# A two-layer streaming encoder step: latents projected among the index scores, index queries in 416 columns, gates and projections placed elsewhere

## The reference

```python
h = rmsnorm(x, g_norm) * (1 + scale) + shift
z = h @ w_in   # cq, ckv, kr, ga, qb, kb, vb, qi, ki, wi, gb, ma, mb
q = (rmsnorm(cq, g_qnorm) @ w_uq)               # latent attention (MLA) queries
kn, va = mla_expand(rmsnorm(ckv, g_kvnorm), w_ukv)
score = jnp.einsum('bqhd,bsd->bqhs', qi, ki)    # index scores, 8 heads
idx_score = jnp.einsum('bqh,bqhs->bqs', wi, relu(score))
vals, idx = lax.top_k(idx_score, topk)          # 128 (prompt), 136 (sample)
# sparse attention (DSA) over the picked keys, with a position bias
ya = (oa * silu(ga)) @ w_oa
yb = (ob * silu(gb)) @ w_ob
m = sigmoid(ma) * ya + sigmoid(mb) * yb
x = x + gate * (m @ w_out)
```

## Time and profile before

| | us |
|---|---|
| median of 3 runs | 1218.14 (1218.10 to 1225.27) |
| the profiled execution | 1217.27 |
| its span, first to last instruction | 1215.4 |
| outside the span | 1.9 |
| mean granted PE clock (1 = 2.4 GHz) | 0.962 |

### The profile page before, as it was taken

How to read it: one execution, slowest core, us unless ns; L and a number is a source line. 1 busy time by engine, 2 the same in 40 slices (tenths; PEclk the granted TensorE clock), 3 DMA queues, 4 the chain that set the end, 5 groups by cost and what they waited for, 6 DMA issues and landing times.

```text
span 1215.4 us, 20113 instructions
## 1 busy us (share of the span) xinstructions
PE 1143.7 (94%) x7828; PEld 994.8 (82%) x7828; DVE 672.1 (55%) x1546; ACT 477.2 (39%) x1088; POOL 347.4 (29%) x213
## 2 busy tenths in 40 slices
PE   8999999999999999899979899999999999989995
PEld 5786995878888888699979499687888888878995
DVE  2828997742367764345363799954336622224535
ACT  3535345433433334323253634533244333333331
POOL 0430733121122222234343073403012321223431
PEclk9997999999999999999999799999999999998998
DMA  9442222111134333113444012221112411111342
GB/s 363 163 149 95 87 71 66 62 36 36 35 101 165 135 138 133 58 37 129 164 153 123 33 56 84 67 77 36 36 35 70 157 53 53 53 52 53 109 161 74
DMA packets 36670, 114.22 MB, mean 94 GB/s; under 512 B 5592, under 2 KB 8248, under 8 KB 35680
## 3 DMA queue, kind: packets, MB, share of 16 engines
q1 hardware_dynamic: 35264, 110.43, 27.5%
q10 hardware_dynamic: 1312, 2.51, 0.6%
HBM read 105.80 MB, written 7.12 MB: 93 GB/s over the span
## 4 chain that ended last, share of the span: by engine, by line
PE 81%; DVE 9%; ACT 5%; issue 2%; DMA 1%; POOL 1%; SPq 0%; POOLq 0%; DVEq 0%; ACTq 0%
PE pj L724 18%; PE pj L726 17%; PE pj L725 17%; PE po L1019 5%; PE ps L963 4%; PE turned L991 3%; PE ps L954 2%; PE pj L908 2%; DVE wide L1579 1%; ACT w_hi L1121 1%; POOL w_lo L1901 1%; PE ps L966 1%; PE pj L882 1%; DMA bias_p<-in_wts 1%; PE ps L836 1%
## 5 line engine op out<-in xcount | busy, mean ns | idle before, releaser
L724 PE MATMUL pj<-h_hi,w_hi 128*128 128x272 f32 x1704 | 506.4, 297 | 4.5 <-POOL w_lo L1901 3.6
L726 PE MATMUL pj<-h_lo,w_hi 128*128 128x272 f32 x1704 | 497.7, 292 | 0.0
L725 PE MATMUL pj<-h_hi,w_lo 128*128 128x272 f32 x1704 | 495.1, 291 | 0.0
L1901 POOL TENSOR_TENSOR w_lo<-ring,w_hi 128x1024 fp32r<-128x1024 f32 x107 | 260.2, 2432 | 580.4 <-ACT w_hi L1121 580.2
L724 PEld LDWEIGHTS pj<-h_hi,w_hi 128*128 128x128 f32 x1704 | 326.6, 192 | 8.0 <-POOL w_lo L1901 4.9
L725 PEld LDWEIGHTS pj<-h_hi,w_lo 128*128 128x128 f32 x1704 | 326.7, 192 | 0.2
L726 PEld LDWEIGHTS pj<-h_lo,w_hi 128*128 128x128 f32 x1704 | 325.5, 191 | 0.0
L1121 ACT ACTIVATE w_hi<-ring 128x1024 fp32r<-128x1024 f32 x107 | 113.7, 1062 | 112.7 <-PE pj L726 99.4
L1313 ACT ACTIVATE probs<-logit,negmax 128x128 f32<-128x128 f32 (+2 forms) x68 | 39.1, 575 | 210.4 <-DVE negmax L1650 196.7
L1650 DVE CUSTOM_DVE_ANT_0 logit<-ps,bias_p 128x128 f32<-128x128 f32 (+1 forms) x64 | 31.4, 491 | 148.8 <-PE ps L966 148.7
L1313 ACT ACTIVATE probs<-ps,negmax 128x128 f32<-128x128 f32 (+2 forms) x68 | 36.4, 536 | 142.7 <-DVE negmax L1641 125.6
(11 more groups left out here) (287 smaller groups left out, 1555.5 us busy)
## 6 DMA issues: line engine op xcount, KB each, us to landing
ring<-in_wts SPq DMA_DIRECT2D x150, 512.0 KB, 3.6
wide<-in_xT SPq DMA_DIRECT2D x4, 1088.0 KB, 7.2
wide<-in_wts SPq DMA_DIRECT2D x6, 512.0 KB, 15.7
ring<-in_wts SPq DMA_DIRECT2D x6, 384.0 KB, 2.9
x_between<-wide ACTq DMA_DIRECT2D x8, 272.0 KB, 3.4
wide<-x_between SPq DMA_DIRECT2D x2, 1088.0 KB, 5.7
bias_p<-in_wts SPq DMA_DIRECT2D x4, 512.0 KB, 14.7
bias_p<-bias_rows SPq DMA_DIRECT2D x1, 2048.0 KB, 7.8
```

What stands on the lines that cost most here:

```text
L724: pe.matmul(out, hi, h_hi[:, k, half(b)], start=(k == first), stop=False)
L725: pe.matmul(out, lo, h_hi[:, k, half(b)], start=False, stop=False)
L726: return pe.matmul(out, hi, h_lo[:, k, half(b)], start=False, stop=(k == stop))
L1901: pool.tensor_tensor(lo, w(splits[n]), hi.bitcast(F32), ALU.subtract).then_inc(s_wlo, 1)
```

## The change

1. `qi` is projected for columns 128 to 543 alone: a tile is 24 matmuls of 416 columns in place of 48 of 272 (in layer 1 the first tile comes in 144 and 272 columns). ACT copies each tile in one piece.
2. The 10 latent jobs come among the index steps, one after every third; ACT copies each out three steps later. `ckv` and `cq` tiles come before `ga` in the ring, and POOL splits 8 tiles in a row there (`rest(8)`, before `rest(3)`), followed by the `ga` gates. The cache DMAs keep their place as to number in the queue: behind the fifth load. The position-bias DMAs come behind the load of `ga` 0, the tenth.
3. DVE does 22 of the 48 prompt rounds of `select` within the index steps i = 2 to 4, 10 behind them, then the latents' norms, then the last 16 (the block with 512 keys), then 4 rounds for the sample, the rotary queries and 3 more as before; the other 10 stand at attention steps that have a projection job, one each. ACT waits for all three prompt selections (`s_sel`, 3) before it copies the first `uv`.
4. Behind the index steps PE projects `ga` 0, sums the squares, and projects `ga` 1 to 3. All of `gb` (8 jobs) is done in the attention, so that 18 jobs lie over steps 0 to 32.
5. `BARE`: steps 59, 61, 63, 65 and 67 have no job, and the 32 `ma`/`mb` jobs reach to step 70; steps 68, 69 and 70 have one each. `output_hi` of gate_a follows the last two `mb` jobs, `output_lo` of gate_a comes behind the loop, the modulation arithmetic goes to step 64, and the output jobs all come behind the loop, with `ya` ordered by halves. The split of `wo` 0 gets the room of `kx_split`, so that `wo` 2 need not wait for `wo` 0.

The diff, cut to its core; the indentation is reduced:

```diff
+BARE = (59, 61, 63, 65, 67)
...
-    t += [("ga", n, P, 1024) for n in range(4)] + [("ckv", n, P, 1024) for n in range(2)]
-    t += [("cq", n, P, 1024) for n in range(3)] + [("gb", n, P, 1024) for n in range(4)]
+    t += [("ckv", n, P, 1024) for n in range(2)] + [("cq", n, P, 1024) for n in range(3)]
+    t += [("ga", n, P, 1024) for n in range(4)] + [("gb", n, P, 1024) for n in range(2)]
...
+    sparse = [s for s in range(FIRST_DSA, len(attention_steps()) + 3) if s not in BARE]
     for i, j in enumerate(jobs):
-        places.setdefault(FIRST_DSA + i - dense if i >= dense else i * (FIRST_DSA - 2) // (dense - 1), []).append(j)
+        places.setdefault(sparse[i - dense] if i >= dense else i * (FIRST_DSA - 2) // (dense - 1), []).append(j)
...
-    f = [("gb", t, b) for t in range(EARLY_GB, 4) for b in range(2)]
+    f = [("gb", t, b) for t in range(4) for b in range(2)]
...
-    j = [("kx", 0, 0), ("qi", 0, 0), ("kx", 0, 1)] if layer else [("kx", 0, 0), ("kx", 0, 1), ("qi", 0, 0)]
-    j += [("qi", t, b) for t in range(1, 4) for b in range(2)]
+    j = [("kx", 0, 0), ("kx", 0, 1), ("qi", 0, 1)]
+    j += [("qi", t, 1) for t in range(1, 4)]
     j += [("vb", 0, b) for b in range(2)]
-    for k, n in (("ga", 4), ("ckv", 2), ("cq", 3), ("gb", EARLY_GB)):
+    for k, n in (("ckv", 2), ("cq", 3), ("ga", 4)):
         j += [(k, t, b) for t in range(n) for b in range(2)]
...
-    j = [(k, f, b) for k in ("ya", "yb") for f in range(2) for b in range(2)]
+    j = [(k, f, b) for k in ("ya", "yb") for b in range(2) for f in range(2)]
...
+def scored(b=None):
+    return slice(P if b != 1 else HF, HF if b == 0 else NT)
...
+        latents = [(k, t, b) for k, n in (("ckv", 2), ("cq", 3)) for t in range(n) for b in range(2)]
...
-            if layer == 0 and (kind, t) == ("ckv", 0):
+            if layer == 0 and (kind, t) == ("ga", 0):
...
-            out = bank(job)
+            cols = scored() if kind == "qi" else half(b)
+            out = bank(job)[:, 0:cols.stop - cols.start]
...
-            for b in range(2 if t else 0):
-                project(("qi", t, b))
+            if t:
+                project(("qi", t, 1))
...
+            if n % 3 == 2:
+                project(latents[n // 3])
...
-        for kind, n in (("ga", 4), ("ckv", 2), ("cq", 3)):
-            for t in range(n):
-                for b in range(2):
-                    project((kind, t, b))
+        for b in range(2):
+            project(("ga", 0, b))
...
-        for t in range(EARLY_GB):
+        for t in range(1, 4):
             for b in range(2):
-                project(("gb", t, b))
+                project(("ga", t, b))
...
-            if s >= NS:
-                output(wo_order()[s - NS])
-        for job in wo_order()[3:]:
+        for job in wo_order():
             output(job)
...
-            for b in range(2):
-                job = ("qi", t, b)
-                if (t, b) == (0, 1):
-                    act.wait_ge(s_q01, at(s_q01, 1))
-                src = ps[:, 0, :] if (t, b) == (0, 1) else full(job)
-                act.activation(qi[:, t, half(b)], src[:, 0:HF], ACT.Copy).then_inc(s_iq, 1)
-                act.wait_ge(s_iq, at(s_iq, 2 * t + b + 1))
-                if (t, b) != (0, 1):
-                    act.sem_inc(s_free[no(layer, job) % 3], 1)
+            job = ("qi", t, 1)
+            act.activation(qi[:, t, scored()], full(job)[:, 0:NT - P], ACT.Copy).then_inc(s_iq, 1)
+            act.wait_ge(s_iq, at(s_iq, t + 1))
+            act.sem_inc(s_free[no(layer, job) % 3], 1)
...
+        def latent(j):
+            kind, t, b = job = latents[j]
+            dst = (ckv if kind == "ckv" else cq)[:, t, half(b)]
+            act.activation(dst, full(job)[:, 0:HF], ACT.Copy).then_inc(s_lat, 1)
+            act.wait_ge(s_lat, at(s_lat, j + 1))
+            act.sem_inc(s_free[no(layer, job) % 3], 1)
+            if b:
+                prepare()
+        def latent_square(n):
+            if n >= 3:
+                act.wait_ge(s_lst, at(s_lst, n - 2))
+            act.activation(squares[:, n % 3, :], (ckv[:, n, :] if n < 2 else cq[:, n - 2, :]), ACT.Square).then_inc(s_lsq, 1)
...
+            if n % 3 == 2 and n > 2:
+                latent(n // 3 - 1)
+        latent(len(latents) - 1)
...
-        for t in range(4):
-            for b in range(2):
-                gate(("ga", t, b))
-            prepare()
         act.wait_ge(s_iac, at(s_iac, len(isteps)))
-        for n in range(5):
-            kind, t = (("ckv", n) if n < 2 else ("cq", n - 2))
...
-            act.activation(squares[:, n % 3, :], dst, ACT.Square).then_inc(s_lsq, 1)
-        act.wait_ge(s_lst, at(s_lst, 2))
+        for n in range(3):
+            latent_square(n)
+        for b in range(2):
+            gate(("ga", 0, b))
+        prepare()
+        for n in range(3, 5):
+            latent_square(n)
...
-        for t in range(EARLY_GB):
+        for t in range(1, 4):
             for b in range(2):
-                gate(("gb", t, b))
+                gate(("ga", t, b))
...
+        act.wait_ge(s_sel, at(s_sel, 3))
...
-            if job[2]:
+            if job[2] and job != ("mb", 7, 1):
                 prepare()
+            if job == ("mb", 5, 1):
+                prepare()
+            if job[0:2] == ("mb", 7):
+                if not job[2]:
+                    act.wait_ge(s_oev, at(s_oev, gate_a_uses))
+                output_hi(gate_a, 0, range(4), job[2], s_gahi)
...
-        for s in range(NS + 2):
+        for s in range(NS + 4):
             if s < NS:
                 exp(s)
-            if s >= 2:
+            if 2 <= s < NS + 2:
...
+        def select_some():
+            for i in (1, 2, 3):
+                if picked[i] < TOPK_P // 8:
+                    return select(i, 1, end=picked[i] + 1 == TOPK_P // 8)
...
-        for i in (1, 2, 3):
-            select(i, TOPK_P // 8)
+            if i > 1 and not (i == 3 and h % 4 == 3):
+                select_some()
+        for _ in range(10):
+            select_some()
...
-        select(4, TOPK_S // 8 - 7, end=False)
+        for i in (1, 2, 3):
+            if picked[i] < TOPK_P // 8:
+                select(i, TOPK_P // 8 - picked[i])
+        select(4, 4, end=False)
...
-            if s == NS - 1:
-                output_lo(gate_a, 0, 0, s_gahi, s_galo)
...
-            if 2 <= s < 6:
-                select(4, 1, end=(s == 5))
+            if s >= 2 and s in fill_at and picked[4] < TOPK_S // 8:
+                select(4, 1, end=(picked[4] + 1 == TOPK_S // 8))
...
```

More of the change, by code:

```diff
@@ L96, in layer_tiles @@
     need = {("uvs", 0): attention_steps().index(("ms", 1, 0)) + 2}
-    for tile, before in zip(used[2:] + [("wo", 0), ("wo", 1)], used):
+    for tile, before in zip(used[2:], used):
         need[tile] = second[before] + 1
+    need["wo", 0], need["wo", 1] = (second[tile] + 1 for tile in used[-3:-1])
     for i, n in enumerate(ada_tiles(layer)):
@@ L325, in w @@
             return ring[:, place[tile] % RING, :]
[L327 removed]
+        own_slot = [(l, k, n) for l, k, n in splits if (k, n) not in (("kx", 0), ("wo", 0), ("wx", 0)) and not (l and (k, n) == ("qi", 0))]
         slot_no = {tile: i for i, tile in enumerate(own_slot)}
@@ L1045, in output @@
                                 pe.wait_ge(s_gblo, at(s_gblo, 4 * b + k - 3))
-                            last = three(out[:, 0:HF], ("wo", f), k, b, start, start + 3)
+                            last = three(out[:, 0:HF], ("wo", f), k, half(b), start, start + 3)
                         last.then_inc(s_full, 1)
@@ L1943, in _ @@
                         rest()
-                    rest(5)
-                    for t in range(EARLY_GB):
-                        for b in range(2):
-                            gate(gate_b, t, b)
-                        rest()
                     pool.wait_ge(s_lno, at(s_lno, 1))
```

103 lines of the change are left out of this document (45 added, 58 removed).

## The result

| | before | after |
|---|---|---|
| median, us | 1216.82 (11 runs) | 1230.12 (1225.5 to 1235.97, 11 runs) |
| ratio | | 1.0108, interval 1.0084 to 1.0132 |
| span of the profiled execution | 1215.4 | 1230.3 |

A forecast was written before the change was run, and what follows sets the result against it. PE, busy 1143.7 of 1215.4 us, was taken as the bound, with time gained only where it stands or crawls. 1217.3 + 0.4 (queries) + 5.6 (index steps to attention) - 11.3 (drain) = 1212.0; forecast 1213 us, range 1197 to 1228.

The forecast's parts named there:

- MLA: Attention steps before DSA: four moved gb jobs cost 12.0 us, filled gaps give back 1.3, +10.7 a layer.
- filled gaps: MLA: jobs fill gaps of 0.65 us at steps that end a head, -1.3 us (0 to -7.9).
- The chain of DVE: From index start I: third selection done at I+106.8, fourth uv job at I+107.5 instead of I+117.9, saving 10.4 us.
- my 4.9 us: DVE idle in the index steps: 3.8 us in block i = 1 and 1.1 at the first step of i = 4.
- my 4.6 for three splits: Index sums: three POOL splits cost 1.6, 1.5 and 1.5 us, idle time takes up 1.5, leaving 3.1 a layer.
- my 62.4 us: DVE's chain from the index start: time for all 48 prompt selection rounds, taken from the kernel before.
- The clock behind the wait: Fourth uv job to attention: PE returns from some 14 us of standing at half clock, +2.5 us (1.5 to 3.5).
- Up to the index steps: Queries in 416 columns, mostly lost to a wait for vb: layer 0 -0.5 us, layer 1 +0.9.
- The drain: End of the attention: 3.9 us lost instead of 9.5, -5.6 us a layer, -11.3 in two.
- (b): Rival: index loop stays at clock 0.74, PE's 45 us become 68, +11.4 a layer, 1236 us; 13%.
- (a): Rival: DVE's chain runs tighter, idle shrinks and sums do not meet splits, 6 us a layer, 1201 us; 27%.
- (c): Rival: the drain moves its loss into the bare steps and the pause of ya, +11 us, 1224 us; 12%.

The follow-up runs named there:

- rounds_moved: The changed kernel with the sample's ten rounds kept away from steps after which DVE has a gate or sample MLA product to do; 1228.69 us, 1.0125.
- job_behind_sample: The changed kernel with the sample's rounds moved likewise and one projection job moved from step 13 to step 12; 1226.35 us, 1.0074.
- vb_first: The changed kernel with POOL's split of the vb tile ahead of the key copies that wait for the cache DMAs; 1224.58 us, 1.0053.
- quiet_pool: The changed kernel with POOL's splits of two ckv, three cq and two ga tiles cut to 32 of 1024 columns, timing only; 1220.43 us, 1.0044.

## Why the forecast failed, step by step

I forecast 1213 and 1197 to 1228; measured are 1230. The spans moved by +14.9 us, my sum was -5.3 against the profiled execution. Of the 20.2 us between them, 11.9 are MLA, 10.8 the way to the fourth `uv` job, 3.4 the clock behind it, and the start of layer 1 another 1.4; layer 0's start (3.2) and its DSA (4.1) came out better.

**MLA, the step that failed most.** My +10.7 was 12.0 for the jobs and -1.3 for filled gaps; measured were +16.5. Busy PE rose by 15.3 us (109.1 to 124.4), which is the jobs and 3.3 us of half clock, a term that I had at nothing; idle PE rose by 1.2 (7.9 to 9.1) where I had it fall by 1.3. No gap was filled: PE's waits for DVE's norm, the gaps of rows 9, add up to 2.6 us before and after.

```profile
PE turned L991 <- DVE probs L1663: 2.6, 5, 0.7
```

```profile
PE turned L1004 <- DVE probs L1690: 2.6, 4, 0.7
```

I put "Six more sample rounds of DVE there lie beside 3 us jobs with DVE at 41%: nothing". A share of 41% says nothing of the step at which a gate product is due: one round stood ahead of a product that values waited for, and that wait was 3.03 us with it and 1.47 without. And I did not place the 18 jobs against the sample's steps: none falls on step 12, behind the small matmuls, where a moved job took 2.0 us of half clock away in layer 0. The 12.0 us of jobs themselves were right, and I saw that they had stood in PE's idle time, but charged their move as "nothing more is gained" and never asked what the wait would be worth if they stayed. The run with them back, 1198.5, answers it: the moved jobs cost 12 us a layer of path for nothing, and with them came the clock behind the wait.

**The chain of DVE.** I+106.8 for the third selection; measured 191.80 - 81.13, I+110.7, and 785.23 - 671.62, I+113.6 in layer 1. The picture was right: DVE nearly without gaps from the second block on, PE standing at the fourth `uv` job (11.0 and 11.2 us; I had some 14), ended by ACT behind the selection. The idle time was my 4.9 us, but by luck as to its place: 2.7 us in the block i = 1, 2.2 at the start of the second, none at i = 4, where I had 1.1. Mis-sized was POOL. The sums lost 4.5 us instead of 3.1: my 4.6 for three splits was right, but the 1.5 that I took off, since "idle time takes up 1.5", did not come. And I had left the norms of the latents at their size of before, 11.8 us, though they now meet the splits and gates of `ga`: 13.4 in layer 0 and 16.3 in layer 1. That makes 3.0 of the 3.9 us in layer 0 and 5.9 of the 6.8 in layer 1; the rest, about 1 us, is not assigned. Groups of layer 1, after:

```profile
L1633 DVE SCALAR_TENSOR_TENSOR probs<-probs,g_q,pT 128x544 f32<-128x544 f32 x3 | 4.9, 1689 | 0.0
L1628 DVE SCALAR_TENSOR_TENSOR ckv<-ckv,g_kv,pT 128x544 f32<-128x544 f32 x2 | 3.6, 1856 | 0.0
```

The kernel before had them at 1165 and 782 ns:

```profile
L1611 DVE SCALAR_TENSOR_TENSOR probs<-probs,g_q,pT 128x544 f32<-128x544 f32 x3 | 3.3, 1165 | 0.0
L1606 DVE SCALAR_TENSOR_TENSOR ckv<-ckv,g_kv,pT 128x544 f32<-128x544 f32 x2 | 1.5, 782 | 0.0
```

The mask of the first selection was stretched in both kernels (1.35 us after), so that my 62.4 us held it already:

```profile
L1595 DVE TENSOR_SCALAR sel<-wide 128x256 bf16<-128x256 f32 x1 | 1.6, 1606 | 0.0
```

The Trainium skill (SBUF — State Buffer, "Who interferes with whom") has the rule for sums and latents: a DVE instruction with two SBUF inputs contends with a GpSimd instruction that reads SBUF, and one with a single input does not unless it runs in a 2-port mode. The runs agree: the sums and latents grew, MAX8 did not (561 ns with splits and without). The mask and L1577 have one tensor input and were stretched; they fit the rule only if they run in a 2-port mode, which the page lists as possible for this operation and no run here shows. I applied the rule to the sums and forgot it for the latents.

**The clock behind the wait.** 4.2 us, above my 1.5 to 3.5. PE came back at half clock, as I had it, and was there again from some 217 us on, during 32 records of matmuls of 32 columns. The windows of this second stretch, after the change and with PE kept busy in the wait:

```profile
216.00:228.00 12.00, 12.00 (x61) 11.85 (x62) 7.09 (x16) 1.84 (x5) 0.00 (x0) 0.57 0.41 132
```

```profile
216.00:228.00 12.00, 12.00 (x84) 11.63 (x84) 7.27 (x17) 2.61 (x8) 1.51 (x2) 0.86 0.37 125
```

0.57 over 12 us is 10.3 us at half clock, 0.86 is 3.4. The end of it lies in MLA, some 1.2 us of its 16.5 in layer 0 (132.3 with PE kept busy). That the idle PE caused the second stretch too is not shown: with as long a wait it was as short as with PE kept busy in four other kernels (`rounds_moved`, `job_behind_sample`, `vb_first` and `quiet_pool`, layer 0), and in layer 1 it stayed in part with PE kept busy. The first stretch came with every such wait; what sets the length of the second is open.

**Up to the index steps.** The wait for `vb` exists, 2.3 and 3.8 us (I had some 4), and swallows the queries' saving in layer 1. In layer 0 no half clock followed it, and the cache was there at 71.8 instead of 73.95 us (POOL's first key copy), so that 3.7 us were gained in these two profiles where I had 0.5. The start varies, though: with the old queries I lay at 82.9 to 84.9 us in three kernels, with the new ones at 80.7 to 82.8 in eight, with means 2.3 us apart. A tile costs more than I took: starts 0.19 us apart, 24 x 0.19 = 4.56 and not 4.25.

```profile
66.21 0.35 PE L731 MATMUL pj<-h_hi,w_hi 128*128 128x416 f32 x1
66.40 0.35 PE L732 MATMUL pj<-h_hi,w_lo 128*128 128x416 f32 x1
```

**The drain.** Right in size and mechanism: -5.8 in layer 1 against -5.6 (4.2 to 5.9 in the run of it alone), with no wait above 1.1 us; the -9.7 of layer 0 holds another wait, as shown above; the pause of `ya` 1.09 against 1.3, step 67's 0.88 against 0.9. The bare steps 59 and 63 cost 0.46 each instead of 0.7.

**The rivals.** (b), the index loop at 0.74, is refuted, the loop runs at 1.00:

```profile
81.13:131.84 50.71, 49.33 (x322) 37.86 (x321) 41.17 (x88) 22.22 (x45) 11.98 (x5) 1.00 0.33 105
```

It was mispriced too: 45 us of work at a mean clock of 0.74 take 45/0.74 = 61 us, not 45 x 1.52 = 68, so 4 us a layer beyond DVE's 57 and 1221 us in all. (a) and (c) did not come either: the sums did meet the splits, and the drain gained what I gave it. The outcome was a rival that I didn't have: the chain as I had drawn it but 3.9 and 6.8 us longer, and the moved jobs dearer than their own length.

## What to carry to other kernels

Before work is moved out of a stretch, ask what the new critical chain of that stretch leaves idle: a job taken from under another engine's wait costs its full length wherever PE is the bound (12.0 us a layer here), and PE, idle in its place, comes back at half clock (the stretch behind it was 1.5 to 4.2 us longer here). Place small extra work by what is due next on its engine, not by the engine's share. And when two engines exclude each other, go through every instruction that the move brings together, not only those that it adds.
